# Both scalings ahead of a pair of turns, a second bank for the turned probabilities, and three inverse roots on GpSimd

## The reference, cut to what matters

```python
def even_mixer(hn, ...):
    z = hn @ w_in
    ...
    out_a = causal_attention_blocks(q_a, k_a, v_a, (MLA_NOPE + MLA_ROPE) ** -0.5)
    q_b = rms_norm(z[..., o3:o3 + dw].reshape(B, S, DIL_HEADS, HEAD_DIM), dil_qn)
    k_b = rms_norm(z[..., o3 + dw:o3 + 2 * dw].reshape(B, S, DIL_HEADS, HEAD_DIM), dil_kn)
    ...
    return mixed @ w_out

def odd_mixer(hn, w_in, qn, kn, w_out):
    z = (hn @ w_in).reshape(B, S, 3, MOBA_HEADS, HEAD_DIM)
    q = rms_norm(z[:, :, 0], qn)
    k = rms_norm(z[:, :, 1], kn)
    v = z[:, :, 2]
    o = moba_attention(q, k, v, alibi_slopes(MOBA_HEADS), HEAD_DIM ** -0.5)
    return o.reshape(B, S, ODD_MIX) @ w_out
```

## Time and profile before

| | |
|---|---|
| runs (3) | 1978.98, 1981.92, 1984.27 us; median 1981.92 |
| profiled execution | 1982.58 us, of which the span is 1980.8 |
| busy, share of the span | PE 97%, PEld 80%, DVE 61%, ACT 46%, POOL 84.9 us |
| chain that ended last | PE 84%, DVE 6%, issue 5%, ACT 2% |
| stretch 1349 to 1405 us (even attention) | PE busy 44.02 of 56, DVE 35.48, ACT 33.02, granted clock 0.94, DMA share 0.28 |
| stretch 1660 to 1755 us (odd attention) | PE busy 84.35 of 95, DVE 65.18, ACT 50.56, granted clock 0.98, DMA share 0.30 |

### The profile page before, as it was taken

The page is one execution under the profiler, slowest core; times in us unless marked ns, Lnnn a source line. Parts: engine busy times, 40 slices in busy tenths (PEclk is TensorE's granted clock), DMA queues, the critical chain, the costliest instruction groups (busy, mean ns, idle before and its releaser), DMA issues.

```text
span 1980.8 us, 24400 instructions
## 1 busy us (share of the span) xinstructions
PE 1930.0 (97%) x9160; PEld 1580.7 (80%) x9160; DVE 1210.6 (61%) x1506; ACT 916.7 (46%) x1143; POOL 84.9 (4%) x161
## 2 busy tenths in 40 slices
PE   9999999999999999999999999898899999989999
PEld 7888888887888788788878888686688887668887
DVE  5555776676446654667667555677555476765545
ACT  5443435545443444343553544366444455544433
POOL 2000100000000100000000000100000000000000
PEclk9999999999999999999999999999999999999999
DMA  9565653446554855564345655353365455236542
GB/s 311 191 219 177 219 185 134 164 149 212 191 191 150 268 191 190 189 215 167 136 165 169 213 190 186 126 170 126 135 221 178 161 200 175 94 123 233 170 169 86
DMA packets 201325, 353.51 MB, mean 178 GB/s; under 512 B 7985, under 2 KB 101089, under 8 KB 201249
## 3 DMA queue, kind: packets, MB, share of 16 engines
q1 hardware_dynamic: 195856, 334.85, 49.8%
q0 software_dynamic: 5392, 17.62, 2.9%
HBM read 351.39 MB, written 1.05 MB: 178 GB/s over the span
## 4 chain that ended last, share of the span: by engine, by line
PE 84%; DVE 6%; issue 5%; ACT 2%; DVEq 2%; DMA 0%; POOL 0%; SPq 0%; ACTq 0%; POOLq 0%
PE acc L686 48%; PE aux L686 29%; DVE w_low L2122 2%; PE aux L802 1%; PE aux L701 1%; ACT w_high L1550 1%; PE aux L956 1%; DVE xT_low L2128 0%; ACT buf_k L2005 0%; DVE x_res L2208 0%; DVEq L2174 0%; PE aux L966 0%; DMA w_raw<-ffn_w 0%; PE aux L1002 0%; PE aux L965 0%
## 5 line engine op out<-in xcount | busy, mean ns | idle before, releaser
L2122 DVE TENSOR_TENSOR w_low<-w_raw,w_high 128x2048 fp32r<-128x2048 f32 (+2 forms) x308 | 695.5, 2271 | 423.7 <-ACT w_high L1550 421.0
L1550 ACT CAST w_high<-w_raw 128x2048 fp32r<-128x2048 f32 (+1 forms) x312 | 586.3, 1894 | 431.6 <-PE acc L686 324.3
L686 PE MATMUL aux<-w_high,xT_high 128*128 128x512 f32 x960 | 380.7, 397 | 3.7 <-DVE xT_low L2128 1.9
L686 PE MATMUL aux<-w_high,xT_low 128*128 128x512 f32 x960 | 374.6, 390 | 0.0
L686 PE MATMUL aux<-w_low,xT_high 128*128 128x512 f32 x960 | 373.9, 389 | 0.0
L686 PE MATMUL acc<-w_high,yT_high 128*128 128x512 f32 (+1 forms) x836 | 332.6, 398 | 3.3 <-DVE yT_low L2274 2.3
L686 PE MATMUL acc<-w_high,yT_low 128*128 128x512 f32 (+1 forms) x836 | 327.3, 391 | 0.0
L686 PE MATMUL acc<-w_low,yT_high 128*128 128x512 f32 (+1 forms) x836 | 327.0, 391 | 0.0
L686 PE MATMUL acc<-w_high,xT_high 128*128 128x512 f32 (+2 forms) x752 | 297.4, 396 | 7.0 <-DVE xT_low L2128 3.8
L686 PE MATMUL acc<-w_high,xT_low 128*128 128x512 f32 (+2 forms) x752 | 291.2, 387 | 0.0
L686 PE MATMUL acc<-w_low,xT_high 128*128 128x512 f32 (+2 forms) x752 | 290.9, 387 | 0.0
(11 more groups left out here) (336 smaller groups left out, 1340.6 us busy)
## 6 DMA issues: line engine op xcount, KB each, us to landing
w_raw<-ffn_w SPq DMA_DIRECT2D x174, 512.0 KB
w_raw<-w_ff SPq DMA_DIRECT2D x64, 1024.0 KB
w_raw<-w_in SPq DMA_DIRECT2D x52, 1024.0 KB
w_raw<-ffn_w SPq DMA_DIRECT2D x44, 1024.0 KB
w_raw<-w_branch SPq DMA_DIRECT2D x16, 1024.0 KB
w_raw<-o_w_in SPq DMA_DIRECT2D x12, 1024.0 KB
w_raw<-w_ple_gate SPq DMA_DIRECT2D x8, 1024.0 KB
w_raw<-e_w_in SPq DMA_DIRECT2D x6, 1024.0 KB
```

The costliest lines, as they stand in the source:

```text
L686: last = nc.tensor.matmul(dst, lhs[:, kt, tok], rhs(j), start=(kt == k_first and q == 0), stop=(kt == k_last and q == 2))
L1550: nc.scalar.copy(whi[:, s, 0:size], raw[:, s, 0:size]).then_inc(slot_hi[s], 1)
L2122: V.tensor_tensor(wlo[:, s, 0:size], raw[:, s, 0:size], cast(whi[:, s, 0:size]), ALU.subtract)\
```

## The change

Five edits, in `build`:

1. `turned(n0, h)` names the bank of a turned head: `acc[:, 1, 1]` for odd heads (in the even mixer all but head 5, in the odd mixer from head 9 on), `aux[2]` for the others. A head in the second bank waits only for the copy of the head two before it. `acc_left` makes TensorE wait until the accumulator's former content is copied.
2. TensorE turns both heads of a pair one behind the other; the pieces that stood between the turns follow both. The transposes of k for the dilated heads (`late_T("kbT")`) move from behind head 2's turn to behind the values of pair 1, and three pieces change places.
3. ScalarE copies both heads, then takes both exponentials. It makes the high parts of units 16 and 17 (even; 14 and 15 odd) and of the first feed-forward unit ahead of the copies; unit 15's comes before the copies of k's banks. The odd mixer's ScalarE program changes likewise from pair 4 on.
4. VectorE does both tables, then a unit's low part where there is one, then both scalings. In the even mixer the low parts of units 14 and 15 move ahead of the first tables. The last low part stands behind everything but the last `pair_low`.
5. Three Newton roots (k of the dilated heads; the second halves of q and k in the odd mixer) become one power instruction of 16 columns on GpSimd each. VectorE signals `var_ready`, and waits for `rstd_ready` ahead of the scaling, which in the odd mixer moves a head later for q (from head 2 to 3), with unit 10's low part behind it.

The diff by core, with eight blanks of indent taken off; the odd mixer's pieces merge as the even one's do:

```diff
+def turned(n0, h):
+    if h % 2 and (h != 5 if n0 == 0 else h > MOBA_H // 2):
+        return acc[:, 1, 1, 0:3 * P]
+    return aux[:, 2, 0:3 * P]
 woven_o = aux[:, 3, 0:S]
...
                 inverse_root(ny[:, 0:3 * NT], nv[:, 0:3 * NT], EPS)
+                pool.wait_ge(var_ready, 8 * DEPTH + 2)
+                nc.gpsimd.tensor_tensor(ny[:, 16:32], nv[:, 16:32], minus_half[:, 0:16], ALU.pow)\
+                    .then_inc(rstd_ready, 1)
                 pool.wait_ge(s_ready, DEPTH * H1 + 1)
...
                 pool.wait_ge(heads_ready, 4)
+            elif n_rms == 0:
+                for k in range(2):
+                    pool.wait_ge(var_ready, 8 * DEPTH + 3 + k)
+                    c = slice(16 * k, 16 * k + 16)
+                    nc.gpsimd.tensor_tensor(ny[:, c], nv[:, c], minus_half[:, 0:16], ALU.pow)\
+                        .then_inc(rstd_ready, 1)
             n += 1
...
-        aux_wait(l, 2)
+        dst = turned(n0, h)
+        apart = h % 2 and h > 0 and (h != 5 if n0 == 0 else h > MOBA_H // 2)
+        pe.wait_ge(aux_read[2], n_aux[2].k + (0 if apart else 1))
         pe.wait_ge(a_ready, DEPTH * H1 + n0 + h + 1)
         for c in range(3):
-            last = nc.tensor.transpose(aux[:, 2, c * P:(c + 1) * P], probs(h)[:, c * P:(c + 1) * P], ident[:])
+            last = nc.tensor.transpose(dst[:, c * P:(c + 1) * P], probs(h)[:, c * P:(c + 1) * P], ident[:])
         aux_end(2, last)
...
+    def acc_left(name):
+        p, n = JOB[name]["acc"][0]
+        pe.wait_ge(acc_read[p], acc_n2(p, n) + 2)
     def values_pair(n0, g, v):
...
     even_scores(0)
-    for g in range(n_even // 2):
-        if g == 0:
-            piece("vb", 1, 1, (0,))
-        else:
-            values_pair(0, g - 1, even_v)
+    piece("vb", 1, 1, (0,))
+    even_scores(2)
+    piece("vb", 1, 1, (1,))
+    acc_left("kb")
+    probs_turned(0, 0)
+    probs_turned(0, 1)
+    values_pair(0, 0, even_v)
+    even_scores(4)
+    piece("vb", 1, 1, (2,))
+    probs_turned(0, 2)
+    probs_turned(0, 3)
+    values_pair(0, 1, even_v)
+    even_scores(6)
+    late_T("kbT", 4, kb, 0)
+    probs_turned(0, 4)
+    piece("vb", 1, 1, (3,))
+    probs_turned(0, 5)
+    for g in range(3, n_even // 2):
+        values_pair(0, g - 1, even_v)
         if 2 * g + 2 < n_even:
             even_scores(2 * g + 2)
-        if g < 3:
-            piece("vb", 1, 1, (g + 1,))
-        elif g == 3:
+        if g == 3:
             out_piece("eout", 1, 0, (0, 1))
+            acc_left("kbT")
         elif g == 4:
-            p, n = JOB["vb"]["acc"][0]
-            pe.wait_ge(acc_read[p], acc_n2(p, n) + 2)
+            acc_left("vb")
             out_piece("eout", 0, 1, (0, 1))
         elif g == 5:
-            out_piece("eout", 1, 0, (2,))
+            out_piece("eout", 1, 0, (2, 3))
         elif g == 6:
...
         probs_turned(0, 2 * g)
-        if g == 1:
-            late_T("kbT", 4, kb, 0)
-        elif g == 3:
-            out_piece("eout", 0, 0, (0,))
-        elif g == 4:
-            out_piece("eout", 0, 0, (2,))
-        elif g == 5:
-            out_piece("eout", 1, 0, (3,))
-        elif g == 6:
-            out_piece("eout", 2, 0, (0,))
-        elif g == 7:
-            out_piece("eout", 3, 0, (0,))
         probs_turned(0, 2 * g + 1)
         if g == 3:
-            out_piece("eout", 0, 0, (1,))
+            out_piece("eout", 0, 0, (0, 1))
         elif g == 4:
-            out_piece("eout", 0, 0, (3,))
+            out_piece("eout", 0, 0, (2, 3))
         elif g == 5:
             out_piece("eout", 0, 1, (2,))
-        elif g == 7:
+        elif g == 6:
+            out_piece("eout", 2, 0, (0,))
+            out_piece("eout", 3, 0, (0,))
+        else:
             out_piece("eout", 3, 0, (1,))
...
             odd_scores(2 * g + 2)
-        if g == 5:
+        if g == 4:
+            acc_left("z5")
+        elif g == 5:
             out_piece("oout", 0, 1, (0, 1))
...
         probs_turned(ODD0, 2 * g)
-        if g == 4:
-            out_piece("oout", 1, 0, (0,))
-        elif g == 5:
-            out_piece("oout", 0, 0, (2,))
-        elif g == 6:
-            out_piece("oout", 0, 1, (2,))
-        else:
-            out_piece("oout", 3, 0, (0,))
         probs_turned(ODD0, 2 * g + 1)
         if g == 4:
-            out_piece("oout", 1, 0, (1,))
+            out_piece("oout", 1, 0, (0, 1))
...
     out_end("oout", lambda: values_pair(ODD0, MOBA_H // 2 - 1, odd_v))
...
     copy_banks(l, flat(bv), parts=MLA_D)
+    high_unit(u0 + 15)
     act.wait_ge(k_gains, 1)
     copy_banks(l, flat(bq), parts=MLA_D, gain=0)
-    high_unit(u0 + 15)
...
         act.wait_ge(aux_full[2], n_aux[2].take() + 1)
-        nc.scalar.copy(probs_T(h), aux[:, 2, 0:3 * P]).then_inc(aux_read[2], 1)
+        nc.scalar.copy(probs_T(h), turned(n0, h)).then_inc(aux_read[2], 1)
...
             pair_copy(0, g - 1)
+        if g == 2:
+            copy_T("kbT", bg_flat[:, 0:D], 1)
+        elif g in (4, 5):
+            high_unit(u0 + 12 + g)
+        elif g == 7:
+            split_unit("eout", 0)
         head_copies(0, 2 * g)
-        if g > 3:
-            head_copies(0, 2 * g + 1)
+        head_copies(0, 2 * g + 1)
         if 2 * g + 2 < n_even:
             head_exps(0, 2 * g + 2, -1.0)
-        if g == 1:
-            copy_T("kbT", bg_flat[:, 0:D], 1)
-        if g < 4:
-            head_copies(0, 2 * g + 1)
-        if 2 * g + 3 < n_even:
             head_exps(0, 2 * g + 3, -1.0)
...
             to_sbuf("vb", two(bg_flat[:, 2 * D:3 * D]))
-        elif g in (3, 4):
-            high_unit(u0 + 13 + g)
-        elif g == 6:
-            split_unit("eout", 0)
     pair_copy(0, n_even // 2 - 1)
...
     kb_sq = ln_par[:, 0, :].rearrange("p (g c) -> p g c", c=HD)
-    group_vars(kb_sq, HD, 16)
-    newton(16, 32)
+    group_vars(kb_sq, HD, 16, signal=var_ready)
+    low_unit(u0 + 14)
+    low_unit(u0 + 15)
     for b, k in ((0, 3), (1, 3), (2, 2), (3, 2)):
...
     head_probs(0, 0)
-    late_low = {1: 14, 2: 15, 4: 16, 5: 17}
+    head_probs(0, 1)
     for g in range(n_even // 2):
...
             pair_low(g - 1)
-        head_probs(0, 2 * g + 1)
         if 2 * g + 2 < n_even:
...
         if g == 0:
+            n_root[0] += 1
+            dve.wait_ge(rstd_ready, n_root[0])
             group_scale(kb, kb, None, HD, None, 16, heads_ready)
         elif g in (4, 5):
-            low_unit(u0 + late_low[g])
+            low_unit(u0 + 12 + g)
+        elif g == 7:
+            split_unit("eout", 0)
         if 2 * g + 2 < n_even:
             head_probs(0, 2 * g + 2)
-        if g in (1, 2):
-            low_unit(u0 + late_low[g])
-        elif g == 6:
-            split_unit("eout", 0)
+            head_probs(0, 2 * g + 3)
     n_aux[2].k += n_even
...
     head_probs(ODD0, 0)
-    late_low = {3: 10, 6: 12, 7: 13, 10: 14, 12: 15}
-    for h in range(MOBA_H):
+    late_low = {6: 12, 7: 13}
+    for h in range(MOBA_H // 2):
         if h in (3, 5, 7):
             pair_low((h - 3) // 2)
-        elif h % 2 == 0 and h > 7:
-            pair_low(h // 2 - 1)
-        if h + 2 < MOBA_H:
-            odd_scores(h + 2)
-        if h + 1 < MOBA_H:
-            head_probs(ODD0, h + 1)
+        odd_scores(h + 2)
+        head_probs(ODD0, h + 1)
         if h == 0:
...
             in_sbuf("z1")
-            group_vars(sq_odd[:, 0:D].rearrange("p (g c) -> p g c", c=HD), HD, 0, HD ** -0.5)
-            newton(0, 16)
+            group_vars(sq_odd[:, 0:D].rearrange("p (g c) -> p g c", c=HD), HD, 0, HD ** -0.5,
+                       signal=var_ready)
+        elif h == 3:
+            n_root[0] += 1
+            dve.wait_ge(rstd_ready, n_root[0])
             group_scale(heads_of(bq, 1), heads_of(bq, 1), None, HD, None, 0, heads_ready)
+            low_unit(unit0 + 10)
         elif h == 4:
             in_sbuf("z3")
-            group_vars(sq_odd[:, D:2 * D].rearrange("p (g c) -> p g c", c=HD), HD, 16, 1.0)
-            newton(16, 32)
+            group_vars(sq_odd[:, D:2 * D].rearrange("p (g c) -> p g c", c=HD), HD, 16, 1.0,
+                       signal=var_ready)
         elif h == 5:
+            n_root[0] += 1
+            dve.wait_ge(rstd_ready, n_root[0])
             group_scale(heads_of(bu, 1), heads_of(bu, 1), None, HD, None, 16, heads_ready)
...
             low_unit(unit0 + late_low[h])
-        elif h == 14:
+    head_probs(ODD0, 9)
+    for g in range(4, MOBA_H // 2):
+        pair_low(g - 1)
+        if 2 * g + 2 < MOBA_H:
+            odd_scores(2 * g + 2)
+            odd_scores(2 * g + 3)
+        if g in (4, 5):
+            low_unit(unit0 + 10 + g)
+        elif g == 7:
             split_unit("oout", 0)
+        if 2 * g + 2 < MOBA_H:
+            head_probs(ODD0, 2 * g + 2)
+            head_probs(ODD0, 2 * g + 3)
     n_aux[2].k += MOBA_H
```

## The result

| | before | changed kernel |
|---|---|---|
| median of the runs | 1982.33 us (4 runs, 1978.98 to 1984.27) | 1959.95 us (4 runs, 1958.51 to 1961.46) |
| span of the profiled execution | 1980.8 | 1958.1 |
| stretch 1349 to 1405: PE, DVE, ACT busy, granted clock | 44.02, 35.48, 33.02, 0.94 | 53.05, 39.51, 36.85, 1.00 |
| stretch 1660 to 1755: the same | 84.35, 65.18, 50.56, 0.98 | 92.45, 65.65, 54.54, 1.00 |

The ratio is 0.9889, with a 95% interval of 0.9872 to 0.9906: 22.4 us less, and a time of 1960 was predicted. In the code of the changed kernel the lines are shifted: a turn is L1288, values L1304 to L1308, a product L701, the scaling L2905 and L2908, a copy L2031, a root L656 (even) and L667 (odd).

A forecast was written before the change was run, and what follows sets the result against it. TensorE was taken as the bound, busy 1930.0 of 1980.8 us, so only its idle or lower-clock time could be won. Terms 3.4 + 9.5 + 1.15 + 8.8 = 22.9 took 1982.6 to 1959.7, predicted as 1960, range 1954 to 1968.

The forecast's parts named there:

- Even mixer, rounds 0 to 2: Up to V3 (values of head pair 3): paired turns (transposes of probabilities) and earlier copies bring V3 at 1370.9; 3.4 us won.
- the walk: Hand timeline of TensorE, ScalarE and VectorE by start-to-start steps over both mixers, from which the 22.9 us won was summed.
- the hole of 5.4: VectorE time ahead of the even mixer's first tables: 2.73 us idle plus 2.7 from the Newton steps; hides 4.4 of lows.
- Rounds 3 to 7: Even mixer, V3 to V7 (values of pairs 3 to 7): 19.2 us instead of 28.7; 9.5 won, of which 2.2 by clock.
- Odd mixer, heads 2 to 7: Without the second Newton root on VectorE, k's scaling and the low behind it come earlier: 1.1 to 1.2 us won.
- Head 7 to V7: Odd mixer, to the values of pair 7: 24.5 us instead of 33.32, VectorE the bound for two rounds; 8.8 won.
- The straight line: GpSimd root time drawn through the rows for 2 and 6 columns: about 3.0 us for 16, 3.3 with hand-offs.
- Rival 2: Even mixer: VectorE's second low waits for GpSimd's root, so V0 and all behind it come 1.9 us later: 1962; chance 0.22.
- Rival 3: Both mixers: half is given back, VectorE or ScalarE being 1 us later a round over eight rounds: 1968; chance 0.13.
- rival 4: More is won: the walk of the odd mixer may come out late, and first rounds pick up waits: 1956; chance 0.10.
- rival 5: TensorE waits for GpSimd roots slower than before; 16 us each would eat 22 us, 25 each gives 2000; chance 0.02.
- Rival 6: No change: feed-forward weights come no earlier and TensorE stands for them behind each mixer: 1981; chance 0.03.

The follow-up runs named there:

- late_second: Changed kernel with the second scaling of each pair back at the start of VectorE's next round, in both mixers: 1961.63 us, ratio to before 0.9900.
- new_split_early: Changed kernel with the last weight unit's cast and low ahead of head 15's scaling again, even mixer only: 1965.63 us, ratio to before 0.9927.
- roots_only_odd: Kernel before with only the odd mixer's two inverse roots moved to GpSimd, order as before: 1980.00 us, ratio to before 0.9992.
- units_back: Changed kernel with the lows of the output weights' first two units back in even-mixer rounds 1 and 2: 1963.72 us, ratio to before 0.9909.
- odd_root_twice: Changed kernel with each of the odd mixer's two GpSimd roots worked out twice: 1964.18 us, ratio to before 0.9914.
- old_split_last: Kernel before with only the last unit's cast and low one place later, the low behind the last scaling, both mixers: 1975.41 us, ratio to before 0.9971.

## Why the prediction was right

That the median came within 0.05 of the 1960 forecast is luck: a second set gave 1960.44, and single runs lie between 1958.5 and 1961.5. What can be held against the forecast are its terms, one by one.

Times in "the time of before" are those of after less 0.40, the difference of the anchors.

**Even mixer, rounds 0 to 2.** Predicted V0 1355.49, V1 1359.85, V2 1365.7, V3 1370.9 and 3.4 won; measured 1355.50, 1359.86, 1365.81, 1371.09 and 3.2. The waits that the walk left in (copies and head 5's one bank) are there, 0.55 to 0.62 each. That the units' lows cost nothing holds: VectorE still idles 1.07 ahead of the first tables. But the hole of 5.4 was only large enough because the Newton steps left it: with them back it costs 1.7.

**Rounds 3 to 7.** Predicted 19.2 (its terms, 18.7 and 0.4, make 19.1), measured 1390.81 - 1371.49 = 19.32; one wait of 0.15 at a second turn, where I had left 0.4.

**Odd mixer, heads 2 to 7.** Predicted 1.15 won; first turn to head 7's takes 42.12 against 43.18, 1.06 won. q's late transposes wait 0.19 instead of 0.35, w_low 0.30.

**Head 7 to V7.** Predicted 24.5, measured 24.61. The rounds with a weight unit take 6.23 and 6.22 from V4 to V6, against the 6.24 worked out from VectorE's work; of the 1.0 that such a round is longer than TensorE's work the profile shows 0.54 as waits (0.36 and 0.18), where the forecast had looked for two of about 0.9. VectorE is the bound there now: it is busy for 5.93 of the 6.20 us from 1710.90 on.

**The root.** The straight line gave 3.0 for 16 columns; it took 2.90 twice in the odd mixer. Its slack was 6.15 for q (root at 1674.88, scaling at 1681.03) and 3.5 for k, against 6.2 and 3.4.

**The rule of the Trainium skill** ("SBUF — State Buffer", Who interferes with whom: the later of two such instructions stands for the whole of the other). The measurement decides: in the even mixer GpSimd's root took 4.88 where it takes 2.90 elsewhere, and 1347.44, when the first low was over, plus 2.90 is its end at 1350.3. So the later one stood, as the page has it. But VectorE's second low began 2.2 us behind the first, on time, beside the root, and took its usual time, 2.31. So here the exclusion held GpSimd and not VectorE. Rival 2 is false, and it was false with 9 us more of roots as well.

**The sum.** 22.9 predicted, 23.1 measured from the anchor, 21.0 to 22.4 by the medians. Undone one at a time the five parts cost 8.0 (bank), 5.5 (last unit), 3.2 (first units), 2.9 (roots) and 2.7 (second scaling). That they make 22.2 together proves little: in the even mixer they make 18.0, more than the 12.6 won there, so they overlap; in the odd mixer bank, scaling and roots make 4.0 of 9.8. The odd mixer's last unit was not undone in the new order; by itself in the old order it gave 3.0 there. Nor was the order of the turns and of ScalarE's copies undone by itself. So for the odd mixer the parts are argued from the walk, whose total there (9.95 predicted, 9.8 measured) came out. Rival 3 would have needed VectorE 1 us later a round; late_second is that case in small, and lost 2.7. For rival 4 the walk of head 7 to V7 would have had to come out too long, and it came out 0.1 short; for rival 5 the roots would have had to take 16 us each. Rival 6 is false too: the stretches behind the mixers, with their feed-forward weights, are no longer than before (271.65 against 271.92, 228.91 against 229.36).

**What was right only in size** is the clock. I took 2.2 (even) and 1.4 (odd) as belonging to waits of over 1 us. In the even mixer the tie is shown, the size is not: with the wait of 3.83 a half clock comes back in new_split_early, but for 3.4 us instead of 6.8, and the cost up to V7 is 5.2 where the walk has 3.9 without the clock and 6.1 with it. The odd part is not tied to its waits: roots_only_odd has those of the last rounds and no half clock there. So up to 1.4 of the 23.1 is how the clock happened to fall in the one trace of before. The argument "no idle of over 1 us is left, so it stays at 2.4 GHz" came out, but units_back shows that its converse fails, with 3.06 of idle at 1.00 all through.

## What to carry to other kernels

When a hand walk by start-to-start steps follows the old order to 0.1 us, use it for the new one: it had every stretch here within 0.2 us, and three of the five undone parts within 0.3; one bank cost 0.6 more than worked out. Where the clock fell or did not fall it was further off: 0.6 too much for the last unit in the new order, 1.0 by the traces and 3.5 by the medians too much in the old one, and 1.5 too little for the odd roots done twice. Where two results go through the same engine in turn, put the independent work between the turn and what waits for its copy, and give each its own bank; and put a weight unit's work behind the last scaling that somebody waits for. Compare traces from the last point that the kernels have in common, since identical code ahead of it came out 3 us apart. Part of that scatter goes with the clock (the mean granted clock from 1260 to 1340 was 0.96 in late_second, 0.94 in before and 0.91 in units_back, which has the latest anchor, 1341.69); the rest has no cause shown. Behind that point the clock can differ from one execution to the next as well, so look at the medians beside the traces.

## What the runs showed of the hardware

- **The clock behind a wait.** It fell to half behind idle times of 3.83 (new_split_early) and of 1.69 and 1.11 with 1.1 of work between them (odd_root_twice), and stayed at 1.00 behind 3.06 (units_back). In the odd mixer of old_split_last it was at half behind waits of 0.94 and 1.82, in a place where roots_only_odd, with waits of 0.95 and 1.82 in the same order, stayed at 1.00. Windows of the two kernels, old_split_last first:

```profile
1730.00:1733.00 3.00, 3.00 (x12) 0.50 0.00 0
...
1733.00:1736.00 3.00, 2.56 (x16) 1.00 0.00 0
```

The length of the wait alone doesn't decide; what does stays open.

- **GpSimd beside VectorE.** In these rows a GpSimd step that started while VectorE subtracted two SBUF operands ended late by what was left of the subtraction: the even root by 2.0 us, as above, and, also in the changed kernel, at 1042.76, an addition of 128x2 that takes 0.19 otherwise took 1.21 and ended when VectorE's second low did. In the rows looked at VectorE never waited for GpSimd. A power of -1/2 on GpSimd took longer with more columns: 0.69 for 2, 1.36 for 6, 2.90 for 16.

```profile
1042.76 1.21 POOL L571 TENSOR_TENSOR inverse_root<-sum_sq,epsilons 128x2 f32<-128x2 f32 x1 [8.04 <-ACT buf_u L1724]
...
1039.43 4.49 DVE L2137 TENSOR_TENSOR w_low<-w_raw,w_high 128x2048 fp32r<-128x2048 f32 x2
```
